# Attention's chunks in another order: the last two value chunks at the end, each group's scores later behind its keys

## The reference

```
q, k, v = jnp.split(h @ w_qkv, 3, axis=-1)          # 1024 -> 3 x 1024
...
s = jnp.einsum('bqhd,bkhd->bhqk', qc, kb) * scale + bias
...
p = jax.nn.softmax(s, axis=-1)
return jnp.einsum('bhqk,bkhd->bqhd', p, vb)         # mixer_a, 16 heads of 64
...
a = p[:, 0] - lam_full * p[:, 1]                    # mixer_c: two maps a head,
return jnp.einsum('bhqk,bkhe->bqhe', a, v)          # 8 heads of 2 x 64
...
return o @ w_o
```

## Time and profile before

| | |
|---|---|
| median of 3 runs | 2790.61 us (2789.27 to 2793.54) |
| the profiled execution | 2796.94 us, its span 2794.8 us |
| PE busy | 2659.7 us, 95% of the span |
| DVE busy | 1717.3 us, 61% |
| ACT busy | 1323.6 us, 47% |
| mean granted clock of PE | 0.96 of full speed |
| stages of attention, about | 968 to 1067 us (`mixer_a`), 1953 to 2055 us (`mixer_c`), 2473 to 2572 us (`mixer_a`) |

### The profile page before, as it was taken

One profiled execution on the slowest core, in us unless ns is written; L12 is line 12 of the kernel. 1 busy time (PEld: TensorE's weight loads), 2 busy tenths in 40 slices (PEclk: granted clock), 3 DMA queues, 4 the chain that ended last, 5 costly groups with the idle time before them and its releaser, 6 DMA issues.

```text
span 2794.8 us, 43242 instructions
## 1 busy us (share of the span) xinstructions
PE 2659.7 (95%) x18533; PEld 2487.0 (89%) x18533; DVE 1717.3 (61%) x2222; ACT 1323.6 (47%) x1927; POOL 151.6 (5%) x224
## 2 busy tenths in 40 slices
PE   8779998799999999999998999999889999999999
PEld 7669988689899888999988998998879999888997
DVE  4747845678566555656656665665666666565663
ACT  6445646455454444444435543544444454444542
POOL 2110001000000100000001000000110000010000
PEclk9769999799999999999999999999989999999999
DMA  7136653056576644656655665765436666553663
GB/s 224 61 80 167 184 188 117 16 162 186 166 204 184 201 150 126 182 184 187 182 180 196 167 187 167 204 182 184 141 110 191 194 183 184 186 188 97 182 184 132
DMA packets 566200, 460.39 MB, mean 165 GB/s; under 512 B 10234, under 2 KB 527178, under 8 KB 566010
## 3 DMA queue, kind: packets, MB, share of 16 engines
q1 hardware_dynamic: 560563, 442.08, 53.4%
q0 software_dynamic: 4656, 15.30, 1.9%
q10 hardware_dynamic: 791, 0.25, 0.1%
HBM read 456.50 MB, written 1.10 MB: 164 GB/s over the span
## 4 chain that ended last, share of the span: by engine, by line
PE 85%; DVE 6%; ACT 4%; DMA 2%; issue 1%; POOL 1%; ACTq 0%; DVEq 0%; POOLq 0%
PE ps L788 25%; PE ps L719 15%; PE ps L720 15%; PE ps L721 15%; PE ps L665 3%; PE ps L667 3%; PE ps L666 3%; PE ps L607 1%; ACT whi L1068 1%; DVE wlo L1497 1%; DMA raw<-in_a_w_qkv 1%; PE ps L870 1%; ACT h_hi L1068 1%; POOL st L2164 1%; PE ps L884 1%
## 5 line engine op out<-in xcount | busy, mean ns | idle before, releaser
L1497 DVE TENSOR_TENSOR wlo<-raw,whi 128x2048 fp32r<-128x2048 f32 x420 | 958.5, 2285 | 552.1 <-ACT whi L1068 551.8
L1068 ACT ACTIVATE whi<-raw 128x2048 fp32r<-128x2048 f32 x420 | 801.3, 1913 | 805.7 <-DMA raw<-in_ff_w_in 439.9
L719 PE MATMUL ps<-h_hi,whi 128*128 128x256 f32 x3648 | 1039.9, 285 | 3.7 <-DVE h_lo L1559 3.7
L720 PE MATMUL ps<-h_lo,whi 128*128 128x256 f32 x3648 | 1036.2, 284 | 0.0
L721 PE MATMUL ps<-h_hi,wlo 128*128 128x256 f32 x3648 | 1036.0, 284 | 0.0
L719 PEld LDWEIGHTS ps<-h_hi,whi 128*128 128x128 f32 x3648 | 704.5, 193 | 10.2 <-issue 10.2
L720 PEld LDWEIGHTS ps<-h_lo,whi 128*128 128x128 f32 x3648 | 704.6, 193 | 0.0
L721 PEld LDWEIGHTS ps<-h_hi,wlo 128*128 128x128 f32 x3648 | 704.3, 193 | 0.0
L788 PE MATMUL ps<-whi,hid_hi 128*128 128x512 f32 x880 | 291.4, 390 | 0.0
L788 PE MATMUL ps<-whi,hid_lo 128*128 128x512 f32 x880 | 290.5, 389 | 0.0
L788 PE MATMUL ps<-wlo,hid_hi 128*128 128x512 f32 x880 | 290.5, 389 | 0.0
(11 more groups left out here) (288 smaller groups left out, 2369.2 us busy)
## 6 DMA issues: line engine op xcount, KB each, us to landing
raw<-in_ff_w_in SPq DMA_DIRECT2D x176, 1024.0 KB, 6.1
raw<-in_ff_w_out SPq DMA_DIRECT2D x88, 1024.0 KB, 4.9
raw<-in_ffn_w_in SPq DMA_DIRECT2D x44, 1024.0 KB, 6.0
raw<-in_a_w_qkv SPq DMA_DIRECT2D x24, 1024.0 KB, 5.3
raw<-in_ffn_w_out SPq DMA_DIRECT2D x22, 1024.0 KB, 4.9
raw<-in_w_in SPq DMA_DIRECT2D x20, 1024.0 KB, 5.4
raw<-in_c_w_qkv SPq DMA_DIRECT2D x12, 1024.0 KB, 5.5
raw<-in_w_out SPq DMA_DIRECT2D x8, 1024.0 KB, 5.0
```

The lines of the kernel that those rows point to most:

```text
L719: e.matmul(out, hi, m.h_hi[:, k, :], start=(k == 0), stop=False)
L720: e.matmul(out, hi, m.h_lo[:, k, :], start=False, stop=False)
L1068: return self.nc.scalar.activation(*a, **k)
L1497: self.e.tensor_tensor(chunk_view(m.wlo[:, slot, :], c), chunk_view(m.raw[:, slot, :], c), chunk_view(m.whi[:, slot, :], c).bitcast(F32), ...
```

## The change

Two tables of numbers change, and nothing else.

```
-ATTEND = (("v", 0), ("v", 1), ("q", 0), ("k", 0), ("q", 1), ("k", 1), ("q", 2), ("k", 2), ("v", 2), ("q", 3), ("k", 3), ("v", 3))
+ATTEND = (("v", 0), ("v", 1), ("q", 0), ("k", 0), ("q", 1), ("k", 1), ("q", 2), ("k", 2), ("q", 3), ("k", 3), ("v", 2), ("v", 3))
...
 def scores_at(b):
-    return (4, 6, 8, 11)[b // 2]
+    return (5, 7, 9, 11)[b // 2]
```

## The result

The changed kernel took 2777.43 us (median of 5 runs, 2773.8 to 2780.59), the kernel before 2792.13 us (5 runs, 2789.27 to 2796.76) on the same chip. The ratio is 0.9945, with a 95% interval of 0.9929 to 0.9961: 0.55% faster, about 15.4 us. The forecast was a gain of 16.1 us. In a later set of runs the same kernel gave 2775.0 us and 0.994 (0.9926 to 0.9954).

A forecast was written before the change was run, and what follows sets the result against it. PE, busy 95% of the span, was taken as the bound, so only its waits and low clock could be won. Gains of 14.6 us in `mixer_a` and 1.5 in `mixer_c` take 2790.61 to 2774.5 us; range 2769 to 2783.

The forecast's parts named there:

- The size: Whole kernel: 14.6 us from both `mixer_a` stages, 7.3 each, plus 1.5 from `mixer_c`, 16.1 us in all.
- The start of `mixer_a`: Scores of pair 0 stop waiting; scores of pair 1 wait 1.0 us for a mask; gain 6.0 us a stage.
- The cause that I gave for the start: Start of attention: POOL's bias tables hold DVE 6.75 us, so k0's eviction is late and pair 0's scores wait 4.39 us.
- The tail: End of `mixer_a`: pair 5's values move into PE's idle time, 3.99 us becoming 2.7; each stage ends 1.29 us earlier.
- the tail gets its clock back: Rival, `mixer_a` tail: shorter idle time keeps the clock high, some 3.5 us more a stage, 2767.5 us; chance 0.08.
- `mixer_c`: DVE and ACT set the pace; pair 7's mask 3.2 us earlier, its weighing 0.9; stage wins 0.9 to 3.2, taken 1.5.
- The 18.1 us period: `mixer_c`: 18.12 us from pair 3's mask to pair 5's, with DVE full or waiting for ACT; three such periods assumed.
- the missing blank turn: The turn without scores, chunk 10, where DVE and ACT could catch up, is lost; in `mixer_a` costed at nothing.
- The rule against the sum: At each start, the new 1.0 us wait was costed without a clock fall; the skill's throttling rule says it may cost.

The follow-up runs named there:

- run 4: Kernel before, with DVE's wait for POOL's bias tables (and `mixer_c`'s mixing factor) moved to just ahead of the first mask; 2786.15 us, ratio 0.9977.
- run 5: run 4's kernel, with the eviction of k0 ahead of the split in chunk 3's turn; scores and order as before the change; 2783.62 us, ratio 0.9957.
- run 10: Changed kernel, tables awaited at first mask, `mixer_c`'s odd masks ahead of keep_out, plus POOL starting `mixer_a`'s tables only after three chunks; 2772.05 us, ratio 0.9924.
- run 3: Kernel before, with only the scores of pairs 4 and 5 one turn later (turns 4, 6, 9, 11); 2789.01 us, ratio 0.9989.
- run 7: Changed kernel, with DVE's odd masks ahead of keep_out in both kinds of stage; 2771.98 us, ratio 0.9921.
- run 2: Kernel before, with only the turns of the scores changed (5, 7, 9, 11), chunk order as before; 2776.25 us, ratio 0.9949.
- run 1: Kernel before, with only the changed order of chunks, turns of the scores as before; 2801.45 us, ratio 1.0035.
- run 6: Changed kernel, with the two edits of run 5 (late wait for tables, k0's eviction ahead of the split); 2774.9 us, ratio 0.9926.

## Why the prediction was right, step by step

**The size** was right: 15.4 us by the ratio, 16.1 forecast, and the profiled stages gave 19.2 and 16.4. Each `mixer_a` stage was to win 7.3 us, and won 8.67 and 7.76 in the first profiled execution, 6.92 and 6.71 in the second.

**The start of `mixer_a`.** Mechanism right: the scores of pair 0 do not wait, those of pair 1 wait for a mask behind one more split. The new wait was put at 1.0 us, and was 0.57, 1.04, 1.32 and 1.69 in four starts. They were to start 25.8 us behind the first q chunk (994.2 less 968.43), and started at 25.25, 25.73, 26.00 and 26.37. In the first stage the scores of pair 7 are 7.67 us earlier, in the second 7.35; the sum of start and tail was put at 7.3.

**The cause that I gave for the start was incomplete where it matters.** "POOL's bias tables hold DVE for 6.75 us. The eviction of k0 is therefore late" holds as it stands for `mixer_c` alone. Runs 4 and 5 show a second delay under it in `mixer_a`, the split of chunk 6 behind its transfer. The tables are behind that one too, as run 10 shows, but by way of the transfers and not of DVE's wait. The sum survived since it rested on when k0 is out and when the mask can start, not on what delays them, and that was luck in part. As advice the sentence would have failed: to let DVE ask for the tables later changed the `mixer_a` stages by -1.7 and +0.6 us (run 4), and to make the tables themselves later won nothing (run 10).

**The tail.** 1.29 us for the values of pair 5 was right (1.3 in run 3), and the idle time of 2.7 us too (2.61). The rest of the first stage's gain, 1.0 us, is the clock that did not fall at once: a part of the rival "the tail gets its clock back", priced at 3.5 us a stage. A whole tail at full clock is seen in the first stage of run 7: 3.2 us shorter than its twin.

**`mixer_c`.** 1.5 us taken out of 0.9 to 3.2, measured 2.74 and 2.76. The mask of pair 7 was forecast 3.2 us earlier and is 3.91 (88.0 to 84.1 from the stage's start), its weighing 0.9 and is 1.75 (92.1 to 90.35). Not foreseen: the values of pair 5 wait 2.46 us for keep_out of pair 4. PE's wait for the eviction of q0, foreseen without a size, was 1.56 us. The 18.1 us period was rightly taken as fixed, and run 7 shows what fixed it: with keep_out and its wait for ACT no longer in front of the mask, the period is 16.1 us.

**No loss from the missing blank turn.** In the later turns of `mixer_a` no scores wait for a mask: the five waits of L856 for L1843 are 0.57 and 1.04 in `mixer_a`, and 2.15, 1.25 and 2.36 in `mixer_c`.

**The rule against the sum** asked whether the clock falls behind the new waits. In `mixer_a` it did not, in four starts of the changed kernel (the clock behind was 1.00 each time). In `mixer_c` it did: 0.58 over the 4 us behind the wait of 2.15. It cost nothing that shows there, as run 2 tells: the same wait of 2.15 us was followed by 1.00, its mask of pair 7 started 84.16 us into the stage, the changed kernel's 84.08, and the stages took 95.10 and 95.01 us. DVE sets the pace of that stage. The Trainium skill, "TensorE: Matmul & The Clock Gate", Part 1, has the throttled state as the default, which activity releases, and says that the monitor does not reset when a kernel starts. These rows agree with it in that the length of a wait alone does not say what follows: the one wait of 2.15 us was followed by 0.58 in one execution and by 1.00 in another.

**Which part does it.** The prediction did not divide the gain over the two edits. It is all in the turns of the scores (run 2); the order of chunks by itself costs 9.8 us (run 1), and beside the new turns it changes nothing that can be measured. The half of the change that its title names first is not needed.

## What to carry to other kernels

Here a wait at the start of a chain between two engines was best filled with other work of the waiting engine: to speed up one link (runs 5, 6 and 10) only let the next one be waited for. A named releaser is the last of several delays, so before building on it, ask what else was not ready at that time, two links back. And where one engine sets a stage's pace, look for an instruction that waits for a third engine in front of one that is ready: in `mixer_c` that was worth 5.8 us (run 7), where the change had won 2.7.

## What the runs showed of the hardware

The clock behind a wait of one place is not settled by the length of the wait. I read the granted clock over the 4 us from the start of the scores that had waited. Behind the scores of pair 1 it was 1.00 after all the waits of 0.57 to 1.79 us (thirteen starts). After waits near 2 us it went either way: 1.98 gave 0.57, 2.01 gave 1.00, 2.10 gave 0.68, 2.12 gave 1.00, 2.13 gave 0.60, four times 2.15 gave 0.58, 1.00, 0.58 and 0.70, and 2.16 and 2.23 gave 1.00. After 2.66 it was 0.61, after 2.72 it was 1.00. After waits near 4 us it was low each time: 0.50 after 3.71 and after 4.29, and at the scores of pair 0 it was 0.60 after 3.88 and 0.50 after 4.39. Another place differs: at the scores of pair 4 in `mixer_c`, waits of 1.62 us gave 0.70 in the kernel before and 0.63 in run 4, and waits of 1.63 us gave 0.66 in run 1 and 1.00 in run 5.

Run 7 shows what this is worth inside one execution. Its two `mixer_a` stages took 88.62 and 94.55 us. Of the 5.9 us between them, 3.2 lie in the tail, where the waits are the same and only the clock differs. Another 1.5 lie between the scores of pair 1 and pair 2, where the clock was 1.00 in one and 0.57 in the other, and the last 1.25 are a longer wait at the start (1.98 for 0.73). So about 4.7 us of a stage can hang on the clock, close to a third of this change's gain, and a single execution's stage time must not be read more finely than that.
